# A quarter of the last gate chunk is made for block two behind the first query, from a second load of its weights; the ring's first places are reordered and the residual is put in later

## The chip, the cores and the metric

The kernel runs on one core of a Trainium2 chip (two dies with four cores each; seven cores are idle). The metric is the device time in microseconds (us) of one launch. Engines: TensorE (PE, with its weight loads as PEld), VectorE (DVE), ScalarE (ACT), GpSimd (POOL), SyncE (SP). Everything is float32.

## The reference, cut to what matters

Two layers over 256 tokens of width 1024. Each is a mixer (attention and a two-way state-space scan, each behind a sigmoid gate), then a product-key mixture of experts with 128 chosen experts per token.

```python
for l in range(DEPTH):                                   # 2
    h = rmsnorm(x, norm1_g[l])
    q, k, v, z, xbc, dt_raw, gate_logits = split(h @ w_in[l])
    a_out = attention(q, k, v) @ w_att_br[l]
    m_out = mamba2_bidir(z, xbc, dt_raw, ...) @ w_ssm_br[l]      # has an rmsnorm inside
    g_att, g_ssm = split(sigmoid(gate_logits + gate_b[l]))       # 1024 features each
    x = x + (g_att * a_out + g_ssm * m_out) @ w_out[l]
    hn = rmsnorm(x, norm2_g[l])
    # experts: 8 heads, 16 experts each
    qry = (hn @ wq).reshape(b, s, 8, 2, 128)
    sc = einsum(qry, keys)                               # 128 key scores, twice per head
    top 16 of each half -> 256 sums -> top 16 -> idx (of 16384 experts), gate = softmax
    act = gelu(einsum('btkd,btd->btk', u_tab[idx], hn))
    x = x + einsum('btk,btkd->btd', act * gate, v_tab[idx])
```

## The kernel before

**Layout.** The mixer keeps activations transposed: features on the 128 partitions, the 256 tokens along the free axis. "Block one" is tokens 0 to 127, "block two" tokens 128 to 255. `hT` is the normed input of a stage, transposed, 8 tiles of 128 features. Weights come as chunks of 2 MB over SP's queue into `w_ring`, which has two slots; chunk c's load waits until TensorE has begun chunk c-1 (semaphore `chunk_freed`). A gate chunk holds four tiles of 128 output features; `half(c, u, m)` makes two of them for all 256 tokens, and ScalarE's `gate` takes the sigmoid into `gateT`. `BESIDE` puts halves of gate and z chunks between the steps of the scan. The last of them, `beside("g", 3)`, the second half of chunk `C_GSSM + 1`, stands behind the scan. Then come the sum of squares of the scan's output (`ysq`), four branch chunks (`project`, 128 matmuls), and VectorE's mixing of both branches into `gateT`.

**From the mixer to the experts.** TensorE does the output product of block one (`out_product`, `out_quarter`), transposes the new x (`turn_half`, `turn_quarter`), makes the query tiles of head 0 (`query_tiles(0, 0, ...)`) and their key scores (`key_scores(0, 0)`). VectorE's `first_eight` finds the best eight experts of head 0 from these scores, and with that the first gather can start. Behind it TensorE makes block two's output product, and VectorE adds it to `x_tok` (`add_half(1, 0)`, `add_half(1, 1)`).

**The gathers.** Each of a layer's 128 "pairs" m = 0 to 127 (64 per block) is two gathers of one expert per token: 128 rows of 8 KB (u and v), 1 MB a gather, issued by POOL in order of m. Their targets are places of two gathers each, `ring = [ring_a, w_ring slot 0, ring_d, ring_f, ring_c]`, places 0 to 4. `PLACE[m]` is the place of pair m, and POOL waits for `pair_used` of the pair that had the place before (`LEFT_BY[m]`). A pair then goes through VectorE (`dots`, two products with a sum, in place), ScalarE (`weigh`: gelu, two scalings, two 128x64 diagonals) and TensorE (16 matmul records against these diagonals, accumulated in two banks), which signals `pair_used`. The places lie over weights that are needed first: `ring_d` over `out1`, `ring_c` over `wq0`, `ring_f` over nothing. Hence POOL's waits for `mix_full` 12 and 13 (block two's output product, both halves) and, at pair 6, for the query tiles of block two's first heads.

**Routing meanwhile.** VectorE works out the experts of the next heads between the dots: `route(p)` is a generator of 21 steps, begun at the pairs in `begun_at`, and after each pair some of its steps are taken (6 for m < 4, 5 for m < 13, then 2). `route(1)` is one head and gives pairs 8 to 15, `route(2)` is two heads and gives pairs 16 to 31, so its steps are longer. The queries of later heads are made by TensorE one tile per pair (`LATE`), their scores copied by ScalarE (`scores_out`). All orders are written out by hand: each engine runs its instructions in program order.

## Time and profile before

| what | value |
|---|---|
| median of 3 runs | 2260.21 us (2258.39 to 2262.55) |
| the profiled execution | 2259.84 us, span 2258.0 us |
| granted TensorE clock, mean | 0.889 of full |
| PE busy / DVE busy | 79% / 60% of the span |
| chain that ended last | PE 51%, DMA 33%, DVE 7%, ACT 3% |
| DMA while the experts are gathered | 421 GB/s in 19 of the 40 slices of the span |

The chain that ended last is the first thing to read: it is followed back from the last instruction, so its shares say which work the end of the kernel hung on. The slices of the page show two stages per layer: one with TensorE at nine tenths and DMA about half busy, and one with DMA at 421 GB/s. The layers are alike: the first key scores stand at 475.26 us in the first and at 1594.70 us in the second.

### The profile page before, as it was taken

The page shows a single profiled execution, that of the slowest core. Times are in us where ns is not written, and L with a number is a line of the kernel's source. Part 1 is how long each engine was busy: PE and PEld are TensorE (multiplying, and loading weights), DVE is VectorE, ACT ScalarE, POOL GpSimd, SP SyncE. Part 2 cuts the span into 40 slices and gives each one's busy share as a digit, 9 for nine tenths or more (in the row PEclk, how much of TensorE's full clock was granted, in tenths as well). Part 3 has the DMA queues.
Part 4 walks back from the last instruction along what each step waited for, and adds up shares of the span by engine and source line. Part 5 has one row for each costly group of instructions (what it writes and reads, how often), then busy time and mean ns, then how long its engine had stood idle before and what let it go on. Part 6 is the DMA issues. An engine that isn't in the chain of part 4 may idle for free.

```text
span 2258.0 us, 26885 instructions
## 1 busy us (share of the span) xinstructions
PE 1778.0 (79%) x10128; PEld 1092.5 (48%) x10128; DVE 1350.3 (60%) x3237; ACT 734.2 (33%) x2049; POOL 605.4 (27%) x600
## 2 busy tenths in 40 slices
PE   8999999997666665555599999999976656655555
PEld 7688888863322211111186888888633222111111
DVE  3377377158776576564525674761686766676644
ACT  2143365024333223322312434540243233232223
POOL 1000002024443443343310000110344444434332
PEclk9999999999988867777799999999989888767867
DMA  5434454769999999999953335547899999999997
GB/s 205 149 116 146 149 218 157 289 267 421 421 421 421 421 421 421 421 422 421 376 179 130 133 132 184 190 154 284 319 421 421 421 421 421 421 421 421 421 421 319
DMA packets 92050, 706.57 MB, mean 313 GB/s; under 512 B 10864, under 2 KB 10992, under 8 KB 17424
## 3 DMA queue, kind: packets, MB, share of 16 engines
q0 software_dynamic: 79712, 554.87, 59.6%
q1 hardware_dynamic: 11488, 146.33, 17.7%
q10 hardware_dynamic: 720, 3.67, 0.5%
q8 instruction: 79, 1.29, 0.2%
q14 instruction: 51, 0.42, 0.0%
HBM read 702.59 MB, written 1.18 MB: 312 GB/s over the span
## 4 chain that ended last, share of the span: by engine, by line
PE 51%; DMA 33%; DVE 7%; ACT 3%; issue 2%; POOL 2%; POOLq 0%; SPq 0%; DVEq 0%; ACTq 0%
PE bank L500 24%; DMA ring_c<-in_peer_uv,ex_i 21%; PE bank L834 7%; DMA w_ring<-in_peer_uv,ex_i 7%; PE bank L476 5%; DVE ring_c L1769 3%; DMA ring_a<-in_peer_uv,ex_i 3%; PE bank L651 2%; PE bank L540 2%; PE bank L713 2%; PE bank L766 2%; POOL ring_c L1920 2%; DVE w_ring L1769 1%; ACT diag L1164 1%; PE bank L693 1%
## 5 line engine op out<-in xcount | busy, mean ns | idle before, releaser
L500 PE MATMUL bank<-hT,w_ring 128*128 128x256 f32 (+1 forms) x2560 | 557.6, 377 | 0.0
L500 PEld LDWEIGHTS bank<-hT,w_ring 128*128 128x128 f32 x2560 | 477.7, 190 | 68.5 <-issue 6.6
L1152 ACT ACTIVATE gel<-act_u 128x2 f32<-128x2 f32 (+1 forms) x258 | 52.4, 203 | 812.8 <-DVE w_ring L1769 168.7
L834 PE MATMUL bank<-ring_a,diag 64*64 64x512 f32 x832 | 140.3, 804 | 97.4 <-ACT diag L1164 97.4
L834 PE MATMUL bank<-ring_c,diag 64*64 64x512 f32 x800 | 135.4, 806 | 93.4 <-ACT diag L1164 93.4
L834 PE MATMUL bank<-w_ring,diag 64*64 64x512 f32 x832 | 134.3, 773 | 93.8 <-ACT diag L1164 93.8
L834 PE MATMUL bank<-ring_f,diag 64*64 64x512 f32 x800 | 133.2, 795 | 91.0 <-ACT diag L1164 90.7
L834 PE MATMUL bank<-ring_d,diag 64*64 64x512 f32 x832 | 135.4, 777 | 84.6 <-ACT diag L1164 84.4
L1920 POOL DMA_INDIRECT ring_a<-in_peer_uv,ex_i x104 | 106.7, 1026 | 310.8 <-DVE ex_i L1689 163.2
L1769 DVE SCALAR_TENSOR_TENSOR ring_a<-ring_a,h 128x1024 f32<-128x1024 f32 x104 | 123.4, 1224 | 87.2 <-DMA ring_a<-in_peer_uv,ex_i 87.0
L1769 DVE SCALAR_TENSOR_TENSOR ring_d<-ring_d,h 128x1024 f32<-128x1024 f32 x104 | 123.5, 1223 | 82.2 <-DMA ring_d<-in_peer_uv,ex_i 81.9
L1769 DVE SCALAR_TENSOR_TENSOR w_ring<-w_ring,h 128x1024 f32<-128x1024 f32 x104 | 123.2, 1222 | 80.5 <-DMA w_ring<-in_peer_uv,ex_i 80.4
L1769 DVE SCALAR_TENSOR_TENSOR ring_c<-ring_c,h 128x1024 f32<-128x1024 f32 x100 | 118.7, 1223 | 84.9 <-DMA ring_c<-in_peer_uv,ex_i 84.6
L1769 DVE SCALAR_TENSOR_TENSOR ring_f<-ring_f,h 128x1024 f32<-128x1024 f32 x100 | 118.6, 1223 | 78.4 <-DMA ring_f<-in_peer_uv,ex_i 78.4
L1164 ACT ACTIVATE diag<-cst,wgt 128x64 f32<-128x64 f32 x510 | 149.9, 340 | 8.4
L1920 POOL DMA_INDIRECT w_ring<-in_peer_uv,ex_i x104 | 112.9, 1086 | 146.0 <-PE bank L834 129.2
L1920 POOL DMA_INDIRECT ring_d<-in_peer_uv,ex_i x102 | 108.5, 1064 | 141.2 <-PE bank L834 116.1
L1920 POOL DMA_INDIRECT ring_c<-in_peer_uv,ex_i x100 | 103.0, 1030 | 155.3 <-PE bank L834 134.4
L1920 POOL DMA_INDIRECT ring_f<-in_peer_uv,ex_i x100 | 103.6, 1036 | 142.4 <-PE bank L834 126.0
L834 PEld LDWEIGHTS bank<-ring_a,diag 64*64 64x64 f32 x832 | 33.0, 164 | 194.9 <-ACT diag L1164 151.1
L1157 ACT ACTIVATE wgt<-gel,gate_w 128x1 f32<-128x1 f32 x510 | 122.8, 287 | 9.5
L834 PEld LDWEIGHTS bank<-w_ring,diag 64*64 64x64 f32 x832 | 31.7, 157 | 185.1 <-ACT diag L1164 144.7
(303 smaller groups left out, 2472.6 us busy)
## 6 DMA issues: line engine op xcount, KB each, us to landing
w_ring<-in_w_stream SPq DMA_DIRECT2D x58, 2048.0 KB, 8.3
fbuf<-cs_rows_dram POOLq DMA_DIRECT2D x32, 512.0 KB, 5.7
wq<-in_w_stream SPq DMA_DIRECT2D x6, 2048.0 KB, 12.7
w_ring<-in_w_stream SPq DMA_DIRECT2D x4, 1024.0 KB, 7.9
out<-in_w_stream SPq DMA_DIRECT2D x2, 2048.0 KB, 15.2
keys<-in_keys_t ACTq DMA_DIRECT2D x2, 1024.0 KB, 4.9
ring_a<-in_peer_uv,ex_i POOLq DMA_INDIRECT x104, 15.4
w_ring<-in_peer_uv,ex_i POOLq DMA_INDIRECT x104, 14.9
```

Of the source, the lines that this page charges most:

```text
L476: ins = pe.matmul(two(b0 + j // 2)[:, j % 2, :], w[:, k, j * P:(j + 1) * P], rhs(k), start=(k == 0), stop=(k == ks - 1))
L500: ins = pe.matmul(two(m % 2)[:, j % 2, cols], w[:, k, (j % 2 if c == 0 else j) * P:((j % 2 if c == 0 else j) + 1) * P], hT[:, k, cols], st ...
L540: ins = pe.matmul(bank[m % 2][:], hT[:, k, b * P:(b + 1) * P], w[:, k, :], start=(k == 0), stop=(k == KD - 1))
L651: ins = pe.matmul(two(2 + i % 2)[:, j, :], w[:, k, col:col + P], attT[:, k, :], start=(k == 0), stop=(k == KD - 1))
L713: ins = pe.matmul(bank[4 + 2 * b + c][:], gateT[:, k, b * P:(b + 1) * P], w[:, k, :], start=(k == 0), stop=(k == KD - 1))
L766: ins = pe.matmul(to[:, j * P:(j + 1) * P], w[:, k, col:col + P], hT[:, k, b * P:(b + 1) * P], start=(k == 0), stop=(k == KD - 1))
L834: ins = pe.matmul(bank[b0 + half_of][n * HB:(n + 1) * HB, :], diag[tokens, PAIR * (m % 2) + s, :], ring[PLACE[m]][tokens, s, DM + n * 512: ...
L1152: act.activation(gel[:, b, c0:c1], act_u[:, b, c0:c1], ACT.Gelu).then_inc(gelu_done.sem, 1)
L1157: ins = act.activation(wgt[:, b, j + s:j + s + 1], gel[:, b, j + s:j + s + 1], ACT.Copy, scale=gates[:, j + s:j + s + 1])
L1164: ins = act.activation(diag[:, PAIR * (m % 2) + s, :], const("blocks"), ACT.Copy, scale=wgt[:, b, j + s:j + s + 1])
L1769: ins = dve.scalar_tensor_tensor(out=row, in0=row, scalar=1.0, in1=h2[:, b, :], op0=ALU.mult, op1=ALU.mult, accum_out=act_u[:, b, PAIR * k ...
L1920: pool.indirect_dma_start(ring[q][:, s, :], None, peer_uv, bass.IndirectOffsetOnAxis(ap=ex_i[:, b, j:j + 1], axis=0))\
```

## The change

The second half of the last gate chunk is made for block one only at its old place (16 matmuls of 128 columns in place of 256). SP loads the same chunk a second time, into a new 2 MB tile `gate_w1` that lies where `ring_a` will be. TensorE makes block two's half of those two tiles (`late_gate`, 16 matmuls) around the first key scores; ScalarE takes its sigmoid into a corner of `sc`, and VectorE (`mix_late`) mixes it into `mixT`, a new tile that holds block two's mixed input of the output product. The two query units of block two's heads 0 and 1 move from pairs 0 to 2 to pairs 6 to 10 (`LATE`). The residual goes into the banks after pair 12 of a block instead of before pair 0.

Pairs 0 to 11 now use four places (3, 0, 1, 2 in turn), and place 4, over `wq0`, is first used by pair 14; from pair 12 on the order is 3, 1, 4, 0, 2. `route(3)` begins at pair 17 instead of 14 and gets three steps a pair.

```diff
-ROUTE_FILLS = [... ("s", 0, 0), ("t", 0, 1), ("q", 2, 0), ("t", 1, 1), ("s", 2, 0), ("q", 0, 1), ("s", 0, 1), ("q", 4, 0) ...
+ROUTE_FILLS = [... ("s", 0, 0), ("g", 0, 1), ("t", 0, 1), ("q", 2, 0), ("t", 1, 1), ("s", 2, 0), ("q", 4, 0), ("s", 4, 0), ("q", 0, 1) ...
-LATE = [(4, 0, (1, 2, 3, 4)), (8, 0, (5, 7, 9, 11)), (12, 0, (15, 17, 19, 21)), ...
+LATE = [(4, 0, (1, 2, 3, 4)), (0, 1, (6, 7, 8, 9)), (8, 0, (11, 12, 13, 14)), (12, 0, (16, 17, 19, 21)), ...
-FIRST_PLACES, PLACES = (0, 1, 2, 3), (0, 1, 4, 2, 3)
+FIRST_PLACES, PLACES = (3, 0, 1, 2, 3, 0, 1, 2, 3, 0, 1, 2), (3, 1, 4, 0, 2)
...
@@ SP
                     if c == C_SSM + 2:
                         sync.dma_start(wq0[:], w_stream[CHUNKS * L + C_WQ]).then_inc(wq0_loaded.sem, 16)
+                        sync.wait_ge(ysq_used.sem, ysq_used.at(L, 1))
+                        sync.dma_start(gate_w1[:], w_stream[CHUNKS * L + C_GSSM + 1]).then_inc(late_gate_loaded.sem, 16)
@@ TensorE
-                    cols = slice(P if c == 0 and L > 0 else 0, SEQ)
+                    cols = slice(P if c == 0 and L > 0 else 0, P if c == C_GSSM + 1 and u == 1 else SEQ)
...
+                        if b == 1 and c == 0 and k == 6:
+                            wait(late_mixed, 1, L)
...
-                out_product(1, 0, range(1))
+                pe.wait_ge(late_gate_loaded.sem, late_gate_loaded.at(L, 16))
+                late_gate(2, range(3))
                 pe.wait_ge(peer_loaded.sem, peer_loaded.at(L, 32))
                 key_scores(0, 0)
-                out_product(1, 0, range(1, 8))
+                late_gate(2, range(3, 8))
+                late_gate(3, range(8))
+                out_product(1, 0, range(8))
...
+                        if k == 12:
+                            add_residual()
                         if m == 0:
                             key_scores(2, 0)
+                        if m == 6:
                             wait(bank_empty, FILL["t", 1, 1] + 1, L)
-                            query_tiles(0, 1, range(2))
-                        if m == 1:
-                            query_tiles(0, 1, range(2, 4))
                         if m == 2:
-                            key_scores(0, 1)
@@ ScalarE
                 scores_out(0, 0)
+                act.activation(warm[:], const("ones")[:, 0:1], ACT.Sigmoid)
+                f = FILL["g", 0, 1]
+                wait(bank_full, f + 1, L)
+                act.activation(sc[:, 1, 2, :], bank[f % 4][:, 2 * P:3 * P], ACT.Sigmoid, bias=param("gb", KD + 6, 1))
+                act.activation(sc[:, 1, 3, :], bank[f % 4][:, 3 * P:4 * P], ACT.Sigmoid, bias=param("gb", KD + 7, 1))
+                gate_exp(0)
                 turned(0)
-                gate_exp(0)
@@ VectorE
+                def mix_late():
+
+                    wait(bank_empty, FILL["g", 0, 1] + 1, L)
+                    step(dve.tensor_tensor(sc[:, 1, 2:4], sc[:, 1, 2:4], qryT[:, 1, 2:4], ALU.mult))
+                    dve.tensor_tensor(mixT[:, 6:KD, :], mixT[:, 6:KD, :], sc[:, 1, 2:4], ALU.add).then_inc(late_mixed.sem, 1)
...
                 first_eight()
                 others = other_eight()
+                mix_late()
                 next(others)
+                next(others)
+                softmax(0)
+                dots(0)
                 add_half(1, 0)
-                next(others)
-                dots(0)
                 add_half(1, 1)
-                softmax(0)
...
-                begun_at = {1: 1, 7: 2, 14: 3, 28: 4, 44: 5, 60: 6, 76: 7, 92: 8}
+                begun_at = {1: 1, 7: 2, 17: 3, 28: 4, 44: 5, 60: 6, 76: 7, 92: 8}
...
-                            for _ in range(6 if m < 4 else 5 if m < 13 else 2):
+                            for _ in range(6 if m < 4 else 5 if m < 13 else 3 if m < 24 else 2):
@@ POOL
                         if m == 1:
+                            pool.wait_ge(bank_full.sem, bank_full.at(L, FILL["g", 0, 1] + 1))
+                        if m == 2:
                             pool.wait_ge(mix_full.sem, mix_full.at(L, 12))
-                        if m == 2:
+                        if m == 3:
                             pool.wait_ge(mix_full.sem, mix_full.at(L, 13))
-                        if m == 6:
+                        if m == ALONE + 2:
                             pool.wait_ge(bank_full.sem, bank_full.at(L, FILL["q", 0, 1] + 1))
```

TensorE from the first query (`hT,wq`) to pair 1's reduction, before. `bank<-w_ring,gateT` and `bank<-out_...,gateT` are block two's output product, `keys,qryT` key scores, `cst,x_tok` transposes, `x_tok,cst` the residual, `ring_...,diag` a pair's reduction:

```order
L766 MATMUL bank<-hT,wq_103 128x128 x12
L713 MATMUL bank<-w_ring,gateT 128x512
L777 MATMUL bank<-keys,qryT 128x128 x2
L713 MATMUL bank<-w_ring,gateT 128x512 x7
L713 MATMUL bank<-out_105,gateT 128x512 x5
L740 MATMUL bank<-cst,x_tok 128x128 x4
L713 MATMUL bank<-out_105,gateT 128x512 x3
L766 MATMUL bank<-hT,wq_103 128x128 x16
L740 MATMUL bank<-cst,x_tok 128x128 x4
L821 MATMUL bank<-x_tok,cst 64x512 x4
L834 MATMUL bank<-ring_a,diag 64x512 x8
L777 MATMUL bank<-keys,qryT 128x128 x2
```

The same stretch of the changed kernel:

```order
L786 MATMUL bank<-hT,wq_104 128x128 x12
L768 MATMUL bank<-hT,gate_w_101 128x128 x3
L797 MATMUL bank<-keys,qryT 128x128 x2
L768 MATMUL bank<-hT,gate_w_101 128x128 x13
L722 MATMUL bank<-w_ring,mixT 128x512 x8
L722 MATMUL bank<-out_106,mixT 128x512 x5
L749 MATMUL bank<-cst,x_tok 128x128 x4
L722 MATMUL bank<-out_106,mixT 128x512 x3
L786 MATMUL bank<-hT,wq_104 128x128 x16
L749 MATMUL bank<-cst,x_tok 128x128 x4
L861 MATMUL bank<-ring_f,diag 64x512 x8
L797 MATMUL bank<-keys,qryT 128x128 x2
```

Between the two key scores 13 small matmuls and one more of 512 columns came in, and the residual's four went out.

POOL at pairs 10 to 16 before, each pair two gathers:

```order
L1920 DMA w_ring<-in_peer_uv,ex_i 128x2048 [waits pair_used]
L1920 DMA w_ring<-in_peer_uv,ex_i 128x2048
L1920 DMA ring_c<-in_peer_uv,ex_i 128x2048 [waits pair_used]
L1920 DMA ring_c<-in_peer_uv,ex_i 128x2048
L1920 DMA ring_d<-in_peer_uv,ex_i 128x2048 [waits pair_used]
L1920 DMA ring_d<-in_peer_uv,ex_i 128x2048
L1920 DMA ring_f<-in_peer_uv,ex_i 128x2048 [waits pair_used]
L1920 DMA ring_f<-in_peer_uv,ex_i 128x2048
```

and pairs 12 to 15 of the changed kernel:

```order
L1968 DMA ring_f<-in_peer_uv,ex_i 128x2048 [waits pair_used]
L1968 DMA ring_f<-in_peer_uv,ex_i 128x2048
L1968 DMA w_ring<-in_peer_uv,ex_i 128x2048 [waits pair_used]
L1968 DMA w_ring<-in_peer_uv,ex_i 128x2048
L1968 DMA ring_c<-in_peer_uv,ex_i 128x2048 [waits bank_full]
L1968 DMA ring_c<-in_peer_uv,ex_i 128x2048
L1968 DMA ring_a<-in_peer_uv,ex_i 128x2048 [waits pair_used]
L1968 DMA ring_a<-in_peer_uv,ex_i 128x2048
```

The first piece is pairs 10 to 13, and pair 13 waits there for pair 8, which had `ring_f` before. In the changed kernel pair 13 goes to `w_ring` and waits for pair 10, and `ring_c` comes behind it.

## Rows read from the trace of the kernel before

**Rows 1.** Chain of waits, first layer: start us, us, what.
```profile
392.60 7.10 PE bank L500 x32
...
474.39 0.86 PE bank L713 x2
475.26 0.45 PE bank L777 x4
475.70 10.30 PE bank L713 x24
...
489.02 3.57 PE bank L766 x32
...
493.03 1.02 PE bank L821 x8
```

**Rows 2.** Stretches: busy us and instructions of each engine; last PEclk, DMA share, GB/s.
```profile
400.00:456.00 56.00, 55.89 (x259) 48.91 (x258) 8.62 (x9) 2.28 (x4) 0.00 (x0) 1.00 0.74 291
...
490.00:500.00 10.00, 10.00 (x92) 7.80 (x94) 6.71 (x27) 4.89 (x17) 5.09 (x6) 1.00 0.98 359
...
520.00:560.00 40.00, 28.70 (x203) 13.38 (x201) 34.10 (x98) 12.97 (x45) 15.00 (x15) 0.87 1.01 421
```

**Rows 3.** Timeline behind the scan: start us, us, engine, line, what.
```profile
394.99 1.27 POOL L1870 TENSOR_TENSOR xbc<-xbc 128x512 f32<-128x512 f32 x1 [1.54 <-ACT xbc L1067]
```

**Rows 4.** Timeline of VectorE, first routings and dots; in brackets idle before, releaser.
```profile
496.86 0.49 DVE L1583 MAX8 vals<-sc 128x8 f32<-128x128 f32 x2 [2.39 <-ACT sc L1121]
...
514.72 1.23 DVE L1769 SCALAR_TENSOR_TENSOR w_ring<-w_ring,h 128x1024 f32<-128x1024 f32 x1 [1.53 <-DMA w_ring<-in_peer_uv,ex_i]
...
524.68 1.23 DVE L1769 SCALAR_TENSOR_TENSOR ring_d<-ring_d,h 128x1024 f32<-128x1024 f32 x1 [2.12 <-DMA ring_d<-in_peer_uv,ex_i]
...
526.98 0.87 DVE L1583 MAX8 vals<-sc 128x8 f32<-128x128 f32 x4
...
539.63 1.30 DVE L1769 SCALAR_TENSOR_TENSOR ring_a<-ring_a,h 128x1024 f32<-128x1024 f32 x1
...
544.88 1.22 DVE L1769 SCALAR_TENSOR_TENSOR w_ring<-w_ring,h 128x1024 f32<-128x1024 f32 x1
...
554.49 1.23 DVE L1769 SCALAR_TENSOR_TENSOR ring_f<-ring_f,h 128x1024 f32<-128x1024 f32 x1 [0.59 <-DMA ring_f<-in_peer_uv,ex_i]
...
559.48 1.23 DVE L1769 SCALAR_TENSOR_TENSOR ring_a<-ring_a,h 128x1024 f32<-128x1024 f32 x1 [2.61 <-DMA ring_a<-in_peer_uv,ex_i]
```

**Rows 5.** Timeline of ScalarE around pair 6 of the first layer.
```profile
518.48 1.28 ACT L1130 ACT_TABLE_LOAD   x1
...
520.30 0.60 ACT L1110 ACTIVATE qryT<-bank 128x512 f32<-128x512 f32 x1 [0.22 <-PE bank L766]
...
523.46 0.58 ACT L1121 ACTIVATE sc<-bank 128x512 f32<-128x512 f32 x1
```

**Rows 6.** Timeline of POOL: pair 2, the last of pair 3, pair 13.
```profile
489.29 0.94 POOL L1920 DMA_INDIRECT ring_d<-in_peer_uv,ex_i  x1 [4.92 <-PE bank L713]
...
493.04 1.09 POOL L1920 DMA_INDIRECT ring_f<-in_peer_uv,ex_i  x1 [0.30 <-issue]
...
539.67 0.94 POOL L1920 DMA_INDIRECT ring_f<-in_peer_uv,ex_i  x1 [6.75 <-PE bank L834]
```

**Rows 7.** DMA issues of 489 to 490 and of 493 to 494: us to landing.
```profile
ring_d<-in_peer_uv,ex_i POOLq DMA_INDIRECT x1, 5.4
...
ring_f<-in_peer_uv,ex_i POOLq DMA_INDIRECT x1, 11.7
```

**Rows 8.** Timeline of TensorE: reductions of pairs 9 and 10, the tile between.
```profile
542.36 3.57 PE L834 MATMUL bank<-ring_a,diag 64*64 64x512 f32 x16 [3.00 <-ACT diag L1164]
...
545.86 2.05 PE L766 MATMUL bank<-hT,wq 128*128 128x128 f32 x16
...
547.84 1.95 PE L834 MATMUL bank<-w_ring,diag 64*64 64x512 f32 x16
```

**Rows 9.** A stretch of 2 us, columns as in rows 2.
```profile
542.00:544.00 2.00, 1.64 (x8) 0.56 (x12) 1.93 (x7) 0.31 (x2) 0.00 (x0) 0.57 1.03 430
```

74 lines of the change are left out of this document (49 added, 25 removed).

## The prediction

> **What bounds the kernel now.** I read the page's slices first: two layers, each a TensorE stage and a gather stage at 421 GB/s [rows 2]. Then the chain of waits. In the first stage it is TensorE without a gap: the half of the last gate chunk takes 7.10 us, then come the sums of squares, the branch chunks (TensorE busy 55.89 of 56 us in 400 to 456 [rows 2]), the output products and, at 475.26, the first key scores [rows 1]. In the second stage it is the gathers. From pair 5 on the dots wait for a landing, and the landings are 5 us apart: 514.72 for pair 5, 554.49 for pair 13, 559.48 for pair 14 [rows 4]; (554.49 - 514.72) / 8 = 4.97 us a pair. So all that a layer gains or loses is how much earlier or later the queue delivers, and the reader can take one mark for it: **pair 14's landing, 559.48**. Behind it nothing but the queue counts, for the ring is five places deep there and each pair comes at the queue's pace.
>
> Before that mark the DMA is not always full: 359 GB/s in 490 to 500 [rows 2]. POOL had waited 4.92 us for block two's output product before pair 2 [rows 6].
>
> **The change part by part (first layer; the second is alike).**
>
> *Half a gate chunk less.* The columns go from 256 to 128. A query tile group of 32 records at 128 columns takes 3.57 us [rows 1], so 7.10 becomes about 3.55. But the sums of squares wait for POOL's last add, which ends at 394.99 + 1.27 = 396.26 [rows 3], while TensorE is now there at 392.60 + 3.55 = 396.15. With a tenth or two for the signal the branch chunks begin 3.3 us earlier. The second load of the chunk is 2.1 MB more in a stretch in which the DMA is 0.74 busy [rows 2]: 56 us x 291 GB/s = 16.3 MB become 18.4 MB, 329 GB/s of 421. I cost it at nothing; if that cover failed, a late chunk would cost up to 2.1 MB / 421 GB/s = 5.0 us.
>
> *Around the first key scores.* The output product's first step, 0.86 us [rows 1], gives way to three steps of the late gate, 3 x 3.57 / 16 = 0.67. Key scores: 475.26 - 3.3 - 0.2 = 471.8.
>
> *The late gate comes back as TensorE work before pair 0.* From key scores to the second head's routing before: 475.26 to 496.86, 21.6 us, with VectorE idle for 2.39 of it until ScalarE had copied head 1's scores [rows 4], which hang on TensorE's row. Between them now stand 13 late gate steps more (2.90) and the output product's first step (0.86), and the residual (1.02) is gone [rows 1]. A turn of block two now waits for `add_half(1, 0)`, which VectorE does behind pair 0's dots: about 0.4 more. Sum +3.1. So `route(1)` starts at 471.8 + 21.6 + 3.1 = 496.5, only 0.4 us before the old 496.86: **the head start of 3.5 us has gone back into TensorE's row before VectorE's routing begins.** VectorE's own addition (`mix_late`, two operations) and ScalarE's (a table load, two sigmoids) lie beside this TensorE work. The removed query tiles of pairs 0 and 1 lie on TensorE beside VectorE's routing and shift no mark by themselves.
>
> *Routing of head 1, pairs 1 to 5.* VectorE is busy from 496.86 to 514.72 - 1.53 = 513.19, 16.3 us [rows 4]. Now 496.5 + 16.3 = 512.8, then the dots of pairs 5 and 6 (2.4 each) to 517.6, without waits, since their data land earlier.
>
> *Where `route(2)` can start.* It needs the scores of heads 2 and 3 from ScalarE. There, behind pair 5's diagonals (dots to 515.2, + 1.4 = 516.6), stand a table load 1.28, an exp 0.3, a copy 0.60, a table load 1.28, pair 6's 1.4 and the scores' copy 0.58 [rows 5]: 522.1. It also comes behind pair 7's dots. Pair 7 landed at 524.68 [rows 4]; it gains the 3.5 us and up to 2.4 us of the thin stretch before pair 3, so 518.8 to 521.2, and its dots end at 521.2 to 523.6. I take 523 for the start, 4.0 before the old 526.98.
>
> *Pair 10 used.* From the start of `route(2)` to the end of pair 10's dots VectorE works without a gap: 526.98 to 544.88 + 1.22 = 546.10, 19.1 us [rows 4]. Now 542.1. ScalarE's part takes 1.4, TensorE's 1.95 at full clock [rows 8], POOL 0.3: 545.7.
>
> *Who waits for it.* Before, POOL issued pair 13 at 539.67 [rows 6], because it took the place of pair 8. It landed at 554.49, so it stood nearly 10 us in the queue. Now pair 13 takes the place of pair 10 and cannot be issued before 545.7, and by then the queue is empty: pair 12's last byte lands at (554.49 - 4.97) - 3.5 = 546.0 at the latest, 543.6 at the earliest, and a gather needs 5.4 us from issue to landing even with nothing ahead of it [rows 7]. Pairs 14 to 16 stand behind pair 13 on POOL, although their places are free. **So the DMA idles, and the mark is set anew by the issue of pair 13.**
>
> *Landing after a standstill.* The trace has one: pairs 2 and 3 after POOL's wait. Issued from 489.29 [rows 6], the fourth gather landed at 493.04 + 11.7 = 504.7 [rows 6, 7], 15.4 us after the first issue. The first took 5.4; three more at 2.5 would make 12.9. So pair 14 lands between 545.7 + 12.9 = 558.6 and 545.7 + 15.4 = 561.1. Against 559.48 that is -0.9 to +1.6 us a layer. I take +1.0, nearer to what the trace shows for four gathers than to the ideal.
>
> The Trainium skill, "DMA: Bandwidth & Descriptors", section "Anatomy of one DMA — SWDGE (gpsimd) path", gives a DMA 2.0 us plus its bytes at 436 GB/s. For 1 MB that is 4.4 us, and the trace shows 5.4 for a lone gather [rows 7]. By the page pair 14 would land at 545.7 + 4.4 + 3 x 2.4 = 557.3, and an estimate of the whole by the page's price is 2259.8 - 4.4 = 2255.4.
>
> Other moves: the residual behind pair 12 has slack, since VectorE sets the pace there; `route(3)` at pair 17 with three steps a pair is done at pair 23, and is needed at pair 32.
>
> **Sum.** Two layers at +1.0: 2259.84 + 2.0 = 2261.8. The profiled execution is 0.37 below the median of 2260.21, so the median comes to 2262.2. Between the bounds, -1.8 to +3.2: 2258.4 to 2263.4, and 1 us a layer more on either side for the start of `route(2)`: 2256.5 to 2265.5 is this case's own range.
>
> **The rivals.**
>
> *The ring stays fed (faster).* If VectorE is through with pair 10 some 5 us sooner than I walk it, pair 13 is issued before the queue runs dry and the mark moves by the whole head start: 3.5 us a layer, or 5.9 with the thin stretch before pair 3 filled. Time: 2260.2 - 7.0 = 2253 to 2260.2 - 11.8 = 2248.4, say 2251. For it: VectorE idled 2.39, 1.53 and 2.12 us for others in the old stretch [rows 4]. Against it: none of these lies in the 19.1 us of `route(2)`, where VectorE has no gap, and that stretch alone decides. Chance 0.16.
>
> *Half clock at pair 10 (slower).* TensorE's granted clock fell to 0.57 in 542 to 544, in place of 1.0 [rows 9], after 3.0 us of waiting, and pair 9's reduction took 3.57 us instead of 1.95 [rows 8]. Pair 10's was at full clock only because a query tile of 2.05 us stood before it [rows 8]. Before, nothing waited for it: POOL was far ahead. Now it sets pair 13's issue. If pair 10's own reduction runs at half clock the mark is 1.6 us later; if also pair 9's and the tile behind it (now on pair 9), 3.57 + 3.6 = 7.2 us do not fit between the dots of 9 and of 10, 546.10 - 540.93 = 5.2 us apart, and 2.0 more come on top. Per layer +1.0 + 1.6 to +1.0 + 3.6, together 2260.2 + 5.2 to 2260.2 + 9.2: 2265.4 to 2269.4, say 2267. It decides from the point at which pair 10's reduction ends later than 545.4. Against it: the moved query tiles sit on pairs 6 to 9, so TensorE has more to do there than before. The Trainium skill, "TensorE: Matmul & The Clock Gate", section "HAM oscillation — how this bites in real kernels", has TensorE slow after waits for DMA in just this shape; by that rule the tiles would help only where they close the waits. Chance 0.23.
>
> *The head start isn't there.* POOL's spans are rough; if its last add ends a microsecond later, the branch chunks start 1 us later, and with them every step to pair 10: +1 us a layer. That is inside the forecast's own range, and I give it no case of its own.
>
> **How the numbers follow.** Forecast 0.61, fed ring 0.16, half clock 0.23. A measurement of this kernel can tell about 0.2%, 4.5 us, from no change: faster is below 2255.7, slower above 2264.7. Of the forecast's 0.61 I count 0.03 below, 0.50 within and 0.08 above; the fed ring is 0.15 faster; of the half clock 0.18 slower, 0.05 within. Faster 0.18, same 0.56, slower 0.26. The range takes the forecast's whole own range and reaches to most of the half clock's and the edge of the fed ring's: 2254.5 to 2268.5. It leaves out some 0.13 below and 0.04 above.
>
> **What would show it.** First key scores at about 471.8. `route(1)`'s first MAX8 at about 496.5, for which VectorE waits. `route(2)`'s first MAX8 near 523. A long wait of POOL for `pair_used` before pair 13 (`w_ring`), and DMA well below 421 GB/s for 3 to 5 us near 545: this is the step on which all hangs. Without that hole the fed ring is right; with it and a reduction of 3.5 us for pair 10, the half clock. The forecast is wrong too if weights are late in the branch chunks, to be seen as TensorE waiting for `w_ring` between 397 and 456.

## The result, and the profile after

The changed kernel takes 2263.6 us, the median of 20 runs (2261.47 to 2267.93), against 2260.39 for 20 runs of the kernel before (2258.18 to 2264.62): ratio 1.0014, interval 1.0008 to 1.0020. That is 3.2 us slower. It is less than the 4.5 us that I called no change, but the interval excludes a gain. The profiled execution took 2262.8 us, span 2261.0, granted clock 0.897 (before 0.889). Its own gate work starts 0.56 us earlier in the record than before's (the full half of the gate chunk ahead of the changed one: 383.04, before 383.60), so 0.56 us is added to the changed kernel's times, and taken from its leads, wherever I say that the record's start is taken out.

The chain of waits in the first layer (start us, us, what), against [rows 1]:

```profile
392.04 3.77 PE bank L507 x32
...
470.36 0.67 PE bank L768 x6
471.03 0.64 PE bank L797 x4
471.67 2.90 PE bank L768 x26
474.57 11.16 PE bank L722 x26
...
492.76 1.88 PE bank L861 x16
```

The half chunk takes 3.77 instead of 7.10, the key scores stand at 471.03 (before 475.26), and the late gate's remaining 2.90 us stand right behind them.

The stretches (busy us and instructions of each engine; last PEclk, DMA share, GB/s), the first three against [rows 2]:

```profile
400.00:456.00 56.00, 56.00 (x252) 47.66 (x251) 8.09 (x16) 0.00 (x0) 0.00 (x0) 1.00 0.81 320
490.00:500.00 10.00, 8.30 (x71) 5.22 (x71) 7.04 (x25) 3.12 (x12) 3.59 (x4) 1.00 0.96 370
520.00:560.00 40.00, 31.39 (x218) 17.20 (x219) 30.97 (x90) 10.16 (x38) 18.50 (x16) 0.87 0.92 364
546.00:548.00 2.00, 2.00 (x20) 0.93 (x12) 1.96 (x5) 0.00 (x0) 0.40 (x1) 1.00 0.23 94
548.00:550.00 2.00, 0.38 (x4) 0.19 (x2) 2.00 (x6) 0.69 (x4) 1.70 (x2) 1.00 0.42 66
```

In 520 to 560 the gathers moved 364 GB/s instead of 421: (421 - 364) x 40 us = 2.3 MB, 5.4 us of the queue. The hole of 546 to 550 is 1.4 MB of it; two smaller dips stand beside it (365 and 254 GB/s in 538 to 542, where pair 12 had waited 5.53 us for pair 8, and 332 and 365 in 550 to 554). "Hole" is used below for the stretch in which the queue of gathers has next to nothing to do.

Timeline of VectorE, against [rows 4]: route(1), pair 7, route(2), pairs 13 and 14:

```profile
495.73 0.49 DVE L1628 MAX8 vals<-sc 128x8 f32<-128x128 f32 x2 [2.72 <-ACT sc L1148]
...
522.57 1.23 DVE L1814 SCALAR_TENSOR_TENSOR ring_d<-ring_d,h 128x1024 f32<-128x1024 f32 x1 [3.29 <-DMA ring_d<-in_peer_uv,ex_i]
...
524.86 0.87 DVE L1628 MAX8 vals<-sc 128x8 f32<-128x128 f32 x4
...
556.92 1.22 DVE L1814 SCALAR_TENSOR_TENSOR w_ring<-w_ring,h 128x1024 f32<-128x1024 f32 x1 [5.24 <-DMA w_ring<-in_peer_uv,ex_i]
...
562.64 1.23 DVE L1814 SCALAR_TENSOR_TENSOR ring_c<-ring_c,h 128x1024 f32<-128x1024 f32 x1 [3.34 <-DMA ring_c<-in_peer_uv,ex_i]
```

The mark, pair 14's landing, stands at 562.64 (before 559.48). Up to pair 12 the dots had been 2.2 us earlier than before; at pair 13 they are 2.4 us later. Timeline of POOL (against [rows 6]): pair 2, pair 13, pair 15:

```profile
489.02 0.94 POOL L1968 DMA_INDIRECT ring_d<-in_peer_uv,ex_i  x1 [4.76 <-PE bank L722]
...
547.60 1.27 POOL L1968 DMA_INDIRECT w_ring<-in_peer_uv,ex_i  x1 [6.81 <-PE bank L861]
...
552.90 0.94 POOL L1968 DMA_INDIRECT ring_a<-in_peer_uv,ex_i  x1 [0.30 <-issue]
```

Pair 13 waited 6.81 us for a reduction (pair 10's), and what stood behind it then went out without a wait. DMA issues of 547 to 548 and of 550.2 to 551, us to landing (against [rows 7]):

```profile
w_ring<-in_peer_uv,ex_i POOLq DMA_INDIRECT x1, 5.9
...
ring_c<-in_peer_uv,ex_i POOLq DMA_INDIRECT x1, 9.1
```

TensorE, reductions of pairs 9 and 10 and the tile between (against [rows 8]):

```profile
540.17 1.95 PE L861 MATMUL bank<-ring_a,diag 64*64 64x512 f32 x16 [0.66 <-ACT diag L1191]
542.04 2.05 PE L786 MATMUL bank<-hT,wq 128*128 128x128 f32 x16
545.35 1.95 PE L861 MATMUL bank<-w_ring,diag 64*64 64x512 f32 x16 [1.25 <-ACT diag L1191]
```

Both reductions took 1.95 us at a granted clock of 1.00 (2.4 GHz): the half-clock rival didn't happen at this place.

### The profile page after: what moved, and what is told of

It is laid out like the page before. It is cut to its first block, busy times and chain, and to the rows that moved or that the text cites. A ratio compares the mean times of both kernels' runs of the same rounds, so it can differ in the third digit from the quotient of the medians.

```text
span 2261.0 us, 27045 instructions
## 1 busy us (share of the span) xinstructions
PE 1777.0 (79%) x10192; PEld 1096.0 (48%) x10192; DVE 1351.6 (60%) x3253; ACT 737.8 (33%) x2057; POOL 604.2 (27%) x600
## 4 chain that ended last, share of the span: by engine, by line
PE 50%; DMA 33%; DVE 9%; ACT 3%; POOL 2%; issue 2%; POOLq 0%; SPq 0%; DVEq 0%; ACTq 0%
PE bank L507 24%; DMA ring_d<-in_peer_uv,ex_i 23%; PE bank L861 7%; DMA ring_a<-in_peer_uv,ex_i 6%; PE bank L483 5%; DVE ring_d L1814 4%; PE bank L658 2%; PE bank L547 2%; PE bank L722 2%; POOL ring_d L1968 2%; DMA ring_f<-in_peer_uv,ex_i 2%; DMA ring_c<-in_peer_uv,ex_i 1%; PE bank L700 1%; ACT diag L1191 1%; DVE ring_a L1814 1%
## 5 line engine op out<-in xcount | busy, mean ns | idle before, releaser
L507 PE MATMUL bank<-hT,w_ring 128*128 128x256 f32 (+1 forms) x2560 | 550.7, 375 | 0.0
L861 PE MATMUL bank<-ring_d,diag 64*64 64x512 f32 x832 | 142.5, 814 | 90.4 <-ACT diag L1191 90.4
L861 PE MATMUL bank<-ring_c,diag 64*64 64x512 f32 x736 | 128.9, 833 | 101.0 <-ACT diag L1191 101.0
L861 PE MATMUL bank<-ring_a,diag 64*64 64x512 f32 x832 | 134.3, 774 | 93.4 <-ACT diag L1191 93.4
L1968 POOL DMA_INDIRECT ring_f<-in_peer_uv,ex_i x106 | 114.2, 1077 | 309.0 <-DVE ex_i L1734 156.2
L1814 DVE SCALAR_TENSOR_TENSOR ring_f<-ring_f,h 128x1024 f32<-128x1024 f32 x108 | 128.2, 1222 | 80.4 <-DMA ring_f<-in_peer_uv,ex_i 79.9
L1814 DVE SCALAR_TENSOR_TENSOR ring_c<-ring_c,h 128x1024 f32<-128x1024 f32 x92 | 109.1, 1223 | 87.3 <-DMA ring_c<-in_peer_uv,ex_i 87.1
L1968 POOL DMA_INDIRECT w_ring<-in_peer_uv,ex_i x104 | 107.5, 1034 | 156.1 <-PE bank L861 136.5
L1968 POOL DMA_INDIRECT ring_c<-in_peer_uv,ex_i x92 | 94.7, 1030 | 143.0 <-PE bank L861 127.9
L861 PEld LDWEIGHTS bank<-ring_d,diag 64*64 64x64 f32 x832 | 33.4, 166 | 182.0 <-ACT diag L1191 138.2
```

What stands on the lines that cost most here:

```text
L507: ins = pe.matmul(two(m % 2)[:, j % 2, cols], w[:, k, (j % 2 if c == 0 else j) * P:((j % 2 if c == 0 else j) + 1) * P], hT[:, k, cols], st ...
L861: ins = pe.matmul(bank[b0 + half_of][n * HB:(n + 1) * HB, :], diag[tokens, PAIR * (m % 2) + s, :], ring[PLACE[m]][tokens, s, DM + n * 512: ...
L1814: ins = dve.scalar_tensor_tensor(out=row, in0=row, scalar=1.0, in1=h2[:, b, :], op0=ALU.mult, op1=ALU.mult, accum_out=act_u[:, b, PAIR * k ...
L1968: pool.indirect_dma_start(ring[q][:, s, :], None, peer_uv, bass.IndirectOffsetOnAxis(ap=ex_i[:, b, j:j + 1], axis=0))\
```

## The experiments

Each recorded expectation below holds a theory and a rival. The first theory was the prediction's: pair 13's wait for pair 10 opens the hole in the queue, and the hole eats the head start. Its rivals: the late gate or another moved piece costs the time by itself. The first four kernels tell these apart.

**p13_on_9**, the changed kernel with one table changed:

```diff
-FIRST_PLACES, PLACES = (...), (3, 1, 4, 0, 2)
+FIRST_PLACES, PLACES = (...), (3, 0, 4, 1, 2)
```

> The changed kernel with the ring's order from pair 12 on 3, 0, 4, 1, 2 in place of 3, 1, 4, 0, 2: pair 13 takes the place of pair 9 instead of pair 10, all else as changed. Theory (the wait of pair 13 for pair 10 empties the queue and that alone eats the head start): pair 9's reduction ended at 542.1 in the changed kernel, so pair 13 is issued near 542.4 instead of 547.6, before the queue is dry; pairs 13 and 14 keep the lead of 2.2 us (first layer) and 3.3 us (second layer, without the first's loss) that pairs 7 to 12 had, so 2260.4 - 5.5 = 2255, between 2253 and 2258. Rival (the loss behind pair 12 comes from other things that were moved, the late residual, route(3)'s three steps a pair, the clock): the order of two places changes nothing, 2262 to 2265.

Measured: 2258.31 us, ratio to before 0.9992 (0.9983 to 1.0001); 5.3 us below the changed kernel. POOL's pair 13, and the two stretches of the hole (94 and 66 GB/s in the changed kernel):

```profile
542.50 1.16 POOL L1968 DMA_INDIRECT ring_a<-in_peer_uv,ex_i  x1 [2.77 <-PE bank L861]
```

```profile
546.00:548.00 2.00, 2.00 (x22) 0.91 (x15) 1.93 (x4) 0.00 (x0) 1.39 (x3) 1.00 1.01 406
548.00:550.00 2.00, 0.46 (x5) 0.26 (x3) 2.00 (x6) 0.65 (x3) 1.70 (x2) 1.00 0.97 406
```

Pair 13 is issued at 542.50 and the queue moves 406 GB/s where it had stood. The hole is worth some 5 us in all, and little else behind pair 12 costs: with the record's start taken out, the first layer's lead is 1.84 us at pair 12 and 1.52 at pair 14. But the time came out 0.3 us above the range that I expected: even with no hole only about 1 us a layer was gained, and the interval does not exclude no gain at all.

**p13_on_11**, the same table as (3, 2, 4, 0, 1).

> The changed kernel with the order 3, 2, 4, 0, 1 from pair 12 on: pair 13 takes the place of pair 11. Theory: pair 11's reduction ended at 553.7, so pair 13 is issued near 554.0 instead of 547.6, and pair 14's landing and the end of each layer come 6.4 us later: 2263.6 + 12.8 = 2276, between 2273 and 2279. Rival (the wait is not what sets the mark): 2262 to 2266.

Measured: 2276.39 us, ratio 1.0065 (1.0050 to 1.0081). Pair 13 is issued at 552.62, 1.4 us sooner than I had put it, and pair 14 lands at 567.18:

```profile
552.62 0.94 POOL L1968 DMA_INDIRECT ring_d<-in_peer_uv,ex_i  x1 [12.07 <-PE bank L861]
```

One pair later in the table is 5.0 us in the issue and 4.5 us at the mark (4.3 and 3.8 with the records' starts taken out), and the hole is longer: 49, 4, 0 and 4 GB/s in the four stretches of 2 us from 546 to 554. The total was right partly by chance: the turn, from the last dots of the first layer to the first MAX8 of the second, took 3.5 us more here (table below).

**ring_alone**, the kernel before with all but the late gate:

```diff
-LATE = [(4, 0, (1, 2, 3, 4)), (8, 0, (5, 7, 9, 11)), (12, 0, (15, 17, 19, 21)), ...
+LATE = [(4, 0, (1, 2, 3, 4)), (0, 1, (6, 7, 8, 9)), (8, 0, (11, 12, 13, 14)), (12, 0, (16, 17, 19, 21)), ...
-FIRST_PLACES, PLACES = (0, 1, 2, 3), (0, 1, 4, 2, 3)
+FIRST_PLACES, PLACES = (0, 1, 2, 3, 0, 1, 2, 3, 0, 1, 2, 3), (0, 2, 4, 1, 3)
...
+                        if k == 12:
+                            add_residual()
```

> The kernel before, without any late gate work and without the second load, but with the rest of the change: four places for pairs 0 to 11, pair 12 behind pair 8 and pair 13 behind pair 10, the two query units at pairs 6 to 10, the residual behind pair 12, route(3) from pair 17. Pair 12 goes to place 0 and 13 to place 2, since place 3 is not free so early without the late gate. Theory: pair 10 is used about 2 us later than in the changed kernel (no head start), pair 13 is issued near 549.5, and the mark is some 5 us later than before, of which 0.7 comes back later: +4.4 a layer, 2260.4 + 8.8 = 2269, between 2266 and 2272. Rival (the late gate is what costs, the ring's order nothing): 2259 to 2262.

Measured: 2270.7 us, ratio 1.0047 (1.0034 to 1.0061), as expected. Pair 13 waited 6.80 us and was issued at 549.64, and pair 14 landed 4.64 us later than before. All that the change does besides the late gate costs 10 us together: the ring's order, the moved query units, the late residual and `route(3)`, which this run doesn't separate. With the late gate 7 us of it come back; 5.7 of these are in the turn between the layers (471.42 against 465.68 us), which is shorter by the second layer's half gate chunk; the granted clock differs there too (table below).

**gate_alone**, the changed kernel with the late gate and the ring and queries nearly as before:

```diff
-FIRST_PLACES, PLACES = (3, 0, 1, 2, 3, 0, 1, 2, 3, 0, 1, 2), (3, 1, 4, 0, 2)
+FIRST_PLACES, PLACES = (3, 0, 1, 2), (3, 0, 1, 4, 2)
...
                         if m == 0:
                             key_scores(2, 0)
-                        if m == 6:
                             wait(bank_empty, FILL["t", 1, 1] + 1, L)
+                            query_tiles(0, 1, range(2))
+                        if m == 1:
+                            query_tiles(0, 1, range(2, 4))
```

> The changed kernel with the late gate kept, but the ring as before in kind (five places deep from pair 8 on, the fifth first used by pair 7), the two query units back at pairs 0 to 2 and route(3) from pair 14. Pair 13 waits for pair 8 again. Theory (the late gate does give a lead, and only the queue's hole takes it): the lead of pairs 7 to 12, 2 to 3.5 us a layer, reaches the end: 2260.4 - 5 = 2255.5, between 2253 and 2257.5. Rival (the work of the late gate between key scores and the second routing eats the head start with any ring): 2259 to 2263.

Measured: 2259.74 us, ratio 0.9996 (0.9987 to 1.0005). This was a miss: my theory had given the late gate 5 us, and the measurement lies with the rival. There is no hole here (422 GB/s in 546 to 550). So the hole is what made the changed kernel slower, but it isn't all: of the first layer's head start of 3.5 us only 0.8 stands at pair 14, even with a ring of the old kind. The second four kernels ask where it goes. The stretches of 4 us show where to look: in p13_on_9 DMA moved 346 and 336 GB/s in 496 to 504 and reached 426 only in 516 to 520, while in the kernel before it was full from 500 on (426 GB/s in 500 to 504).

**gate_rows_out**, p13_on_9 with most of the late gate's matmuls gone:

```diff
-                late_gate(2, range(3))
+                late_gate(2, range(1))
...
-                late_gate(2, range(3, 8))
-                late_gate(3, range(8))
+                late_gate(3, range(1))
```

It leaves out 14 of the 16 matmuls, so block two's half of these two tiles is not the full product.

> The kernel p13_on_9 (pair 13 behind pair 9, 2258.3) with 14 of the 16 matmuls of the late gate left out, so that block two's half of these two tiles is a product over one of eight feature tiles only. 13 of them stood between the first key scores and the output product of block two: 2.9 us. Theory (the late gate's own row before route(1) eats the lead that the shorter chunk gives, and VectorE's routing and the places that its dots set free hand this on to the queue): route(1) starts 2.9 us earlier, and pair 14's landing too, by 2 to 3 us a layer: 2258.3 - 5 = 2253, between 2251.5 and 2255. Rival (in 496 to 516 the queue is held by something that these matmuls don't move, so the row is not what eats the lead): no change, 2257 to 2260.

Measured: 2257.91 us, ratio 0.9988 (0.9980 to 0.9997). The time is the rival's, but not for its reason, for route(1) itself hadn't moved. From the first key scores' MAX8 to route(1)'s it took 23.96 us, in p13_on_9 24.02 (24.7 in both_rows' expectation is the same stretch from the key scores' matmul). The chain of waits says what held it:

```profile
483.40 2.37 DVE ring_f L1813 x4
485.77 0.61 DVE x_tok L1593
486.43 0.66 PE bank L749 x4
```

The changed order of VectorE puts pair 0's dots (2.37) ahead of `add_half(1, 0)` (x_tok), and block two's transposes wait for that. So two rows of equal length run between the key scores and route(1): in p13_on_9 the chain follows TensorE's, here VectorE's.

**fifth_at_6**, gate_alone with PLACES (3, 0, 4, 2, 1).

> The kernel gate_alone with the order 3, 0, 4, 2, 1 from pair 4 on: the fifth place, over wq0, is used by pair 6 (as before) instead of pair 7. In gate_alone pair 6 waited until 509.8 for pair 2, and DMA moved 344, 354, 317 and 379 GB/s in the four stretches of 4 us from 500 to 516, together (77 + 67 + 104 + 42) x 4 = 1.2 MB or 2.8 us less than at 421. Theory (after the head start the queue lacks free places, not time): pair 6 is issued near 504, the hole of 500 to 512 closes, and pair 14 lands 1.5 to 2.5 us earlier a layer: 2259.7 - 4 = 2255.7, between 2254 and 2257.5. Rival (what is won there is lost again at the next wait, pair 7 for pair 3 or pair 8 for pair 2): 2258.5 to 2261.

Measured: 2260.38 us, ratio 0.9997 (0.9988 to 1.0006). The time is the rival's. Pair 6 went out early, pair 7 then waited for pair 3, and a hole opened there:

```profile
505.06 1.47 POOL L1975 DMA_INDIRECT ring_c<-in_peer_uv,ex_i  x1 [1.27 <-PE bank L786]
...
513.89 1.55 POOL L1975 DMA_INDIRECT ring_d<-in_peer_uv,ex_i  x1 [6.12 <-PE bank L861]
```

```profile
512.00:516.00 4.00, 4.00 (x39) 2.39 (x35) 2.60 (x6) 2.15 (x9) 1.80 (x2) 1.00 0.58 244
```

So pair 6's earlier issue (509.80 in gate_alone) was lost at the next wait. Part of this is the table's own doing: it gives pair 7 the place of pair 3 and pair 8 that of pair 2, while the kernel before had them the other way round. Pair 2's reduction ended at 508.65 here, 5.2 us ahead of pair 7's issue. The order 3, 0, 4, 1, 2 would have let pair 7 go then and wasn't run, so this run doesn't show that an earlier fifth place is worth nothing.

**third_load**, p13_on_9 with the second load made twice:

```diff
+                        sync.wait_ge(late_gate_loaded.sem, late_gate_loaded.at(L, 16))
+                        sync.dma_start(gate_w1[:], w_stream[CHUNKS * L + C_GSSM + 1]).then_inc(late_gate_loaded.sem, 16)
```

> The kernel p13_on_9 with the second load of the gate chunk made twice, one behind the other: 2.1 MB more a layer, in the stretch of the branch chunks. Theory (the load has cover there, DMA is 0.8 busy): no change, 2257 to 2259.5. Rival (loads in that stretch delay the chunks behind them): some us a layer, up to 2 x 5 = 2268.

Measured: 2271.88 us, ratio 1.0045 (1.0032 to 1.0058). It is the rival, and 4 us beyond its upper end. The chain shows a load that takes 17 us beside two others, SP waiting for it, and the next chunk issued behind it:

```profile
412.17 17.07 DMA gate_w<-in_w_stream
...
429.63 13.00 DMA w_ring<-in_w_stream
```

TensorE waited 4.2 us for that chunk. My edit did two things: it added a load, and it held SP's queue until 429.26, by 4 us. They aren't separated. What it shows is how thin the cover is. In p13_on_9, with one extra load, the same chunk is issued at 425.21 and takes 8.9 us (8.1 before the change), to 434.1, and TensorE begins it at 439.0. So the second load costs nothing as it stands, with 4.9 us to spare, while the DMA share of the stretch, 0.8, had looked like room for more.

**residual_first**, p13_on_9 with the residual ahead of pair 0 again:

```diff
+                    add_residual()
                     for k in range(BLOCK_PAIRS):
...
-                        if k == 12:
-                            add_residual()
```

> The kernel p13_on_9 with the residual put into the banks before pair 0, as before the change, instead of behind pair 12. Theory: it stands in TensorE's row ahead of pair 0's reduction and head 1's key scores, so route(1) starts 1.0 us later, and of that 0.5 to 1 us reaches the queue: +1 to +2 in all, 2259 to 2261. Rival (the late residual itself costs at pair 12): 2256 to 2258.

Measured: 2259.68 us, ratio 0.9996 (0.9987 to 1.0005), +1.4 on p13_on_9, whose ratio lies within this interval, so the difference of the medians isn't clear of noise. In the trace route(1) comes 24.87 us after the key scores instead of 24.02, and pair 14 0.7 us later: as expected.

**both_rows**, gate_rows_out with VectorE's order around pair 0 as before the change:

```diff
                 mix_late()
                 next(others)
+                add_half(1, 0)
                 next(others)
-                softmax(0)
                 dots(0)
-                add_half(1, 0)
                 add_half(1, 1)
+                softmax(0)
```

> The kernel gate_rows_out (2257.9; 14 of the late gate's 16 matmuls left out) with VectorE's order around pair 0 as before the change: block two's first sum into x (add_half(1, 0)) behind the first step of the other experts, pair 0's dots behind it, the softmax last. Theory (two rows of equal length lie between the first key scores and route(1): TensorE's, which the late gate lengthened, and VectorE's, on which dots(0) and softmax(0) now stand ahead of add_half(1, 0), for which TensorE's turn waits; taking work out of one leaves the other): with both shortened route(1) starts 2 to 3 us earlier after the key scores than the 24.7 us of p13_on_9 and gate_rows_out, and pair 14 lands 1.5 to 3 us earlier: 2257.9 - 4.5 = 2253.5, between 2251.5 and 2255.5. Rival (route(1)'s start is not what the queue's lead hangs on): route(1) earlier but the time at 2256.5 to 2259.

Measured: 2253.08 us, ratio 0.9966 (0.9954 to 0.9978): 4.8 us below gate_rows_out. route(1) came 21.66 us after the key scores, and DMA was full in 496 to 504. First p13_on_9, then both_rows:

```profile
496.00:500.00 4.00, 2.79 (x24) 1.43 (x25) 3.83 (x18) 1.09 (x5) 2.09 (x3) 1.00 0.94 346
500.00:504.00 4.00, 2.03 (x19) 1.31 (x21) 3.86 (x12) 1.27 (x5) 2.29 (x2) 0.99 1.01 336
```

```profile
496.00:500.00 4.00, 3.04 (x28) 2.01 (x20) 3.90 (x12) 0.34 (x2) 2.34 (x2) 1.00 1.02 422
500.00:504.00 4.00, 2.99 (x16) 0.78 (x16) 3.86 (x14) 0.93 (x4) 0.49 (x1) 0.64 1.02 418
```

This is the head start as it would be if the late gate's work cost next to nothing: 3.7 us at the mark. That the end of the two rows hands it on to the queue is shown, and by more than route(1): POOL issues pair 3 at 487.2 instead of 489.9 (it waits for block two's output product) and pairs 4 and 5 at 493.6 and 497.4 instead of 496.4 and 500.1 (they wait for the reductions of pairs 0 and 1), and none of these waits for work that stands behind route(1)'s start. Only the places of pair 6 and later hang on dots behind it. The run doesn't separate the two.

**vector_row**, p13_on_9 with the same edit of VectorE's order and the whole late gate.

> The kernel p13_on_9 (2258.3) with VectorE's order around pair 0 as in both_rows, and the whole late gate. Theory of two rows: TensorE's row is full between the key scores and route(1) here, so shortening VectorE's alone moves route(1) by at most 0.4 us: no change, 2257 to 2259.5. Rival (VectorE's order alone is what holds): route(1) 2 us earlier and 2254 to 2256.

Measured: 2258.09 us, ratio 0.9987 (0.9978 to 0.9996), as expected; route(1) 24.02 us after the key scores, unmoved. Each row alone holds it. Its profiled execution was earlier at pair 14 than p13_on_9 by 1.3 us all the same (table), which the theory of two rows doesn't give and the median doesn't repeat. Most of it is in TensorE's clock at one reduction, that of pair 2, for whose place pair 6 waits. First p13_on_9, then vector_row:

```profile
503.11 2.93 PE L861 MATMUL bank<-w_ring,diag 64*64 64x512 f32 x16 [1.97 <-ACT diag L1191]
```

```profile
504.29 1.95 PE L861 MATMUL bank<-w_ring,diag 64*64 64x512 f32 x16 [1.98 <-ACT diag L1191]
```

In p13_on_9 the granted clock was 0.50 (1.2 GHz) in 504 to 506, in vector_row 1.00 (2.4 GHz), after the same wait; with the records' starts taken out, pair 6 is issued at 506.65 and 505.70. The changed kernel has the slow one too (3.10 us), gate_alone and gate_rows_out the fast one. It isn't the whole account: gate_rows_out issues pairs 6 and 7 when vector_row does, and its pair 7 lands 1.0 us later. A lead below is one profile's, and 1 us in it can be the execution's.

**dots_sooner**, p13_on_9 with one number changed:

```diff
-                            for _ in range(6 if m < 4 else 5 if m < 13 else 3 if m < 24 else 2):
+                            for _ in range(5 if m < 13 else 3 if m < 24 else 2):
```

> The kernel p13_on_9 with 5 steps of route(1) behind pairs 1 to 3 instead of 6 (the rest of them then behind pair 5, where VectorE waited for data). Theory (from 496 to 516 the queue lacks free places, and those come from VectorE's dots): dots of pairs 2 and 3 come 0.6 and 1.2 us earlier, pairs 6 and 7 are issued that much earlier, DMA moves more in 504 to 516, and the lead at pair 14 grows by 0.6 to 1.5 us a layer: 2256.2, between 2255 and 2257.5. Rival (the lead is set elsewhere, or what is won is lost at pair 8, which now waits for route(1)): 2257.5 to 2260.

Measured: 2255.23 us, ratio 0.9979 (0.9970 to 0.9988). p13_on_9 in 508 to 512 (in 512 to 516 it moved 330 GB/s), then dots_sooner in both stretches:

```profile
508.00:512.00 4.00, 4.00 (x35) 2.52 (x35) 3.90 (x9) 0.63 (x4) 2.01 (x2) 1.00 0.97 379
```

```profile
508.00:512.00 4.00, 3.43 (x29) 2.07 (x30) 3.88 (x10) 0.99 (x5) 2.12 (x2) 1.00 1.01 422
512.00:516.00 4.00, 3.62 (x32) 2.06 (x31) 3.71 (x9) 1.07 (x6) 1.22 (x2) 1.00 1.01 426
```

The lead at the mark is 3.0 us instead of p13_on_9's 1.5, as the theory has it. But pair 2's reduction ran at full clock here (1.95 us), and of the 1.4 us by which pair 6 is issued earlier only 0.4 are pair 2's earlier dots. The intervals of the two kernels' ratios overlap as well, so what the steps alone are worth isn't separated.

Two tables of numbers, with no work removed, turn the change into a gain over both kernels: 0.21% against before, 0.35% against the changed kernel (0.9979 / 1.0014).

**both_orders**, dots_sooner with vector_row's edit as well.

> The kernel dots_sooner (2255.2; pair 13 behind pair 9, 5 steps of route(1) a pair) with VectorE's order around pair 0 of vector_row as well, nothing left out. In the profiles vector_row's lead at pair 14, counted from the late gate half's start, was 1.3 us larger than that of p13_on_9, dots_sooner's 1.5 us. Theory (both fill the same thin stretch of the queue, 492 to 516, by different pairs): the two add up in part, 0.3 to 1 us a layer more than dots_sooner alone: 2254, between 2252.5 and 2255.5. Rival (one is enough, the second fills what is already filled, or vector_row's lead in its profile was chance, as its median says): 2254.5 to 2257.

Measured: 2257.25 us (2253.63 to 2263.84), ratio 0.9985 (0.9976 to 0.9994). In the first layer its lead at the mark is the largest of the complete kernels, 0.5 us over dots_sooner, as the theory has it (pair 2's reduction took 1.95 us in both). The time isn't better, and 0.3 us above the rival's range: the turn to the second layer took 3.7 us more in its profiled execution. The intervals of the two overlap, so which of them is faster isn't settled.

**All of them in one table.** The third column is from the first key scores' MAX8 to route(1)'s. Leads (us earlier than before) are those of pair 14's dots in the first layer and of that layer's last, against before, with the record's own start taken out (the full gate half's start against 383.60). The turn is from the last dots of the first layer to the first MAX8 of the second. The last column is the granted clock in 1130 to 1140.

| kernel | median us | key to route(1) | lead at 14 | lead at layer's end | turn | clock |
|---|---|---|---|---|---|---|
| before | 2260.4 | 21.12 | | | 469.66 | 1.00 |
| changed | 2263.6 | 24.02 | -3.7 | -3.0 | 465.68 | 1.00 |
| p13_on_9 | 2258.3 | 24.02 | 1.5 | 1.3 | 465.51 | 1.00 |
| p13_on_11 | 2276.4 | 24.02 | -7.5 | -6.5 | 469.21 | 0.84 |
| ring_alone | 2270.7 | 20.26 | -4.6 | -4.1 | 471.42 | 0.83 |
| gate_alone | 2259.7 | 24.02 | 0.8 | 1.5 | 468.11 | 0.83 |
| gate_rows_out | 2257.9 | 23.96 | 1.2 | 1.9 | 468.70 | 0.83 |
| fifth_at_6 | 2260.4 | 24.02 | 0.7 | 1.0 | 469.51 | 0.83 |
| third_load | 2271.9 | 24.02 | -4.9 | -5.0 | 476.95 | 0.77 |
| residual_first | 2259.7 | 24.87 | 0.8 | 1.2 | 468.17 | 0.83 |
| both_rows | 2253.1 | 21.66 | 3.7 | 4.3 | 465.48 | 1.00 |
| vector_row | 2258.1 | 24.02 | 2.8 | 2.8 | 465.86 | 1.00 |
| dots_sooner | 2255.2 | 24.02 | 3.0 | 2.7 | 465.80 | 1.00 |
| both_orders | 2257.3 | 24.02 | 3.5 | 3.5 | 469.46 | 0.76 |

## Why the prediction was right, point by point

The forecast was 2262.2, with the queue running dry before pair 13. Measured were 2263.6, by that mechanism. That the two times are so close is luck in part, as the points below show.

*Half a gate chunk less: right, somewhat undersized.* I had 3.55 us for the half and 3.3 for the lead at the branch chunks. The half took 3.77 (it ended at 395.8, and no wait for POOL's add followed); the branch chunks began at 396.89 instead of 400.68, 3.2 us with the record's start taken out. In the second layer the turn at full clock is 469.66 - 465.68 = 4.0 us shorter, where "the second is alike" had 3.5.

*The second load at nothing: right,* but I read its cover from the wrong row. The share of DMA in the stretch says little here; what counts is when the next chunk lands, 4.9 us ahead of its use. third_load, which also holds SP's queue, overruns that.

*The key scores at 471.8: 471.03,* or 471.6 with the record's start. *The late gate comes back as TensorE's row, +3.1: right.* Key scores to route(1) grew by 24.02 - 21.12 = 2.9 us; the residual's part is 0.85 of my 1.02 (residual_first). What I missed is the second row. I had laid VectorE's additions "beside this TensorE work" and counted dots(0) ahead of `add_half(1, 0)` as 0.4 us; gate_rows_out showed that VectorE's new order is a row as long as TensorE's. It changes nothing in the sum, and everything in what a cure would be.

*route(2)'s start at 523: too early by 1.9 us (524.86).* The step that failed is pair 7's landing, 518.8 to 521.2, measured 522.57. I let it gain the whole head start and up to 2.4 us of the thin stretch. But the place of pair 4 is set free behind TensorE's row (its issue is 0.6 us earlier than before), and those of pairs 6 and 7 by dots behind a route(1) only 0.6 us earlier, with four places in use where the kernel before had five from pair 6 on. So the queue had nothing to take: 307 GB/s in 496 to 500. The thin stretch wasn't filled, it moved. both_rows shows it the other way round: with the two rows shortened it is full in 496 to 504. In the changed kernel's profile a reduction at the lower clock came on top: pair 2's took 3.10 us instead of 1.95, and pair 6 is issued right behind it, at 506.26. My estimate from the two durations is 1.15 us.

*Pair 10 used: 545.7, measured 547.60,* by those 1.9 us. The span from route(2) to the end of pair 10's dots was 543.92 - 524.86 = 19.1 us, exactly what I had taken from [rows 4].

*The dots of pairs 8 to 12.* I had written that from pair 5 on the dots wait for a landing. Between pair 8 and pair 12 they don't, before or after the change: there VectorE sets the pace, and the landings only show again at pair 13. The pace that I took, 4.97 us a pair, holds all the same, since DMA was full (421 GB/s).

*Who waits for it: right.* The hole is there, 94 and 66 GB/s in 546 to 550, and p13_on_9 and p13_on_11 show by moving the wait one pair either way that it sets the mark: 542.50, 547.60 and 552.62 give leads of 1.5, -3.7 and -7.5.

*Landing after a standstill: inside the bounds, but the upper one rested on a wrong reading.* From pair 13's issue to pair 14's landing it took 15.04 us; I had bounds of 12.9 and 15.4 and took a value worth 14.8. The stretch that gave the 15.4 was no standstill: when pair 2 was issued before the change, DMA was still moving 418 GB/s (488 to 490), and pair 1's second gather landed at 492.0. So its 5.4 us was not the time of a lone gather either. That the value came out is luck. Three real standstills give 15.04 (changed), 14.56 (p13_on_11) and 14.48 us (ring_alone) for the four gathers. The estimate by the price of the Trainium skill, "DMA: Bandwidth & Descriptors", section "Anatomy of one DMA — SWDGE (gpsimd) path", had pair 14 land 4.4 us + 3 x 2.4 = 11.6 us after the issue; the trace has 15.04, and 5.9 us for the lone first gather. The measurement decides against that price here.

*The mark, +1.0 a layer: undersized.* In the first layer it was +3.7 (record's start taken out), of which 0.7 came back by the layer's end, so +3.0. From pair 12 to pair 14 both layers lost the same 5.4 us (from 2.24 earlier than before to 3.16 later, and from 0.85 to 4.53). But in the second layer the turn had given 4.0 instead of 3.5, and 1.6 us came back later: +0.5 for the layer. Together 3.5, less the record's 0.56: the profile's last dots are 2.94 later than before, against 2.0 forecast. Of the first layer's 2.7 us too little at the mark, 1.9 are route(2)'s start, 0.2 the landing and 0.56 the record's start. So the small miss of the total, 3.2 against 1.8 us in the medians, hides a first layer that was off by 2 us and a second that was off by half a microsecond the other way: the sum was helped by errors that cancel.

*The rivals.* "The ring stays fed" was false for the changed kernel, and its price was wrong too. With the ring fed (p13_on_9) the gain was some 2 us in all, not 7 to 12: the head start gets lost a second time, in TensorE's and VectorE's rows ahead of route(1), and I had priced the rival as if only the hole could eat it. "Half clock at pair 10" didn't happen: its reduction took 1.95 us. A half clock cost time at two places of which I hadn't spoken, pair 2's reduction (3.10 us) and, in six kernels of those below, the turn between the layers.

## What to carry to other kernels

When work is moved from before a critical point to behind it, follow every engine's row to the next point where the limiting resource is fed, and ask which row is second: taking the same 2.9 us out of TensorE's row was worth 0.4 us, VectorE's order alone 0.2, and both together 5.2. In a ring the wait that matters is the first one whose release comes later than the queue's last byte; one table entry moved the first layer's mark 5.2 us one way and 3.8 the other. A queue that starts earlier keeps little of it unless its places come free earlier: look at what frees them, and do that first.
